# Attention scores from stacked float32r parts in place of zero-padded float32 operands

## What is computed

```
def _fox_attention(q, k, v, log_f):              # 8 heads of 64, causal, decay F
        s = jnp.einsum('bqhd,bkhd->bhqk', qi, k) * (HEAD_DIM ** -0.5)
        s = s + Fi[..., :, None] - F[:, :, None, :]
        s = jnp.where(kpos <= qpos, s, NEG)
        p = jax.nn.softmax(s, axis=-1)
        return jnp.einsum('bhqk,bkhd->bqhd', p, v)

def _swa_attention(q, k, v, sinks, rel_bias):    # 8 heads of 64, 2 groups of keys, window of 128
    logits = jnp.einsum('bnqhgd,bnkhd->bnhgqk', q, kb) * (HEAD_DIM ** -0.5) + bias
    p = softmax(concat([logits where valid, sink]))[..., :-1]
```

## Time and profile before

| | us |
|---|---|
| median of 3 runs | 3645.55 |
| lowest and highest | 3643.78, 3648.18 |
| the profiled execution's own time | 3645.56 |
| its span | 3643.8 |

### The profile page before, as it was taken

One profiled execution on the slowest core, in us unless ns is written; L12 is line 12 of the kernel. 1 busy time (PEld: TensorE's weight loads), 2 busy tenths in 40 slices (PEclk: granted clock), 3 DMA queues, 4 the chain that ended last, 5 costly groups with the idle time before them and its releaser, 6 DMA issues.

```text
span 3643.8 us, 49395 instructions
## 1 busy us (share of the span) xinstructions
PE 3344.9 (92%) x17315; PEld 2844.1 (78%) x17315; DVE 2569.9 (71%) x4990; ACT 1189.1 (33%) x2308; POOL 1856.8 (51%) x1095
## 2 busy tenths in 40 slices
PE   3999988888978778999999799999999999999997
PEld 3888766776857667888888688888888888888885
DVE  5111046652359998889889688888888887888888
ACT  3112135541122214666666322222222222222222
POOL 3991000004133433333333477777777777777776
PEclk8999989999989989999999899999999999999998
DMA  4443210013222113665666687888888888888885
GB/s 185 129 131 104 75 47 12 12 49 125 104 71 71 51 51 119 244 239 205 235 243 231 242 266 251 262 254 251 261 255 256 256 260 256 250 261 254 253 254 201
DMA packets 405835, 662.49 MB, mean 182 GB/s; under 512 B 219680, under 2 KB 270952, under 8 KB 402928
## 3 DMA queue, kind: packets, MB, share of 16 engines
q1 hardware_dynamic: 324656, 365.05, 31.4%
q0 software_dynamic: 78656, 286.30, 23.8%
q10 hardware_dynamic: 2304, 8.39, 0.6%
HBM read 564.21 MB, written 94.40 MB: 181 GB/s over the span
## 4 chain that ended last, share of the span: by engine, by line
PE 44%; DVE 10%; DMA 5%; POOL 1%; ACT 1%; issue 0%; SPq 0%; DVEq 0%; ACTq 0%; POOLq 0%
PE psum L2154 9%; PE psum L2155 9%; PE psum L2156 9%; PE psum L374 4%; PE psum L373 4%; PE psum L372 4%; DMA g_row<-in_expert_down,rows_of 4%; DVE g_hot L1850 4%; DVE g_hot L1829 2%; DVE g_row L1840 2%; DVE g_hot L1833 2%; POOL ga_downT_lo L1274 1%; PE psum L1282 1%; PE psum L1284 1%; PE psum L1283 1%
## 5 line engine op out<-in xcount | busy, mean ns | idle before, releaser
L2154 PE MATMUL psum<-e_u_hi,e_w_hi 128*128 128x512 f32 x1536 | 599.9, 391 | 16.7 <-POOL e_w_lo L2378 16.7
L2155 PE MATMUL psum<-e_u_lo,e_w_hi 128*128 128x512 f32 x1536 | 599.4, 390 | 0.0
L2156 PE MATMUL psum<-e_u_hi,e_w_lo 128*128 128x512 f32 x1536 | 598.6, 390 | 0.0
L2244 DVE TENSOR_TENSOR acc<-acc,psum 128x512 f32<-128x512 f32 x508 | 342.4, 682 | 248.0 <-PE psum L2156 232.9
L2260 DVE SCALAR_TENSOR_TENSOR acc<-e_row,e_row_weights,acc 128x1024 f32<-128x1024 f32 x256 | 468.7, 1831 | 10.2 <-DVE acc L2260 0.5
L2385 POOL TENSOR_TENSOR e_u_lo<-e_up,e_u_hi 128x1024 fp32r<-128x1024 f32 x128 | 388.8, 3038 | 16.3 <-ACT e_u_hi L2184 14.4
L2378 POOL TENSOR_TENSOR e_w_lo<-e_table,e_w_hi 128x768 fp32r<-128x768 f32 x128 | 247.4, 1933 | 249.9 <-ACT e_w_hi L2188 248.9
L2372 POOL DMA_INDIRECT e_row<-in_expert_up,rows_of x256 | 329.1, 1286 | 65.8 <-issue 53.3
L2154 PEld LDWEIGHTS psum<-e_u_hi,e_w_hi 128*128 128x128 f32 x1536 | 289.3, 188 | 75.7 <-POOL e_w_lo L2378 17.3
L2156 PEld LDWEIGHTS psum<-e_u_hi,e_w_lo 128*128 128x128 f32 x1536 | 289.1, 188 | 60.7
L2155 PEld LDWEIGHTS psum<-e_u_lo,e_w_hi 128*128 128x128 f32 x1536 | 289.4, 188 | 57.9
(11 more groups left out here) (277 smaller groups left out, 7919.5 us busy)
## 6 DMA issues: line engine op xcount, KB each, us to landing
e_up<-in_expert_up SPq DMA_DIRECT2D x128, 512.0 KB, 4.4
gate_table<-g_table SPq DMA_DIRECT2D x12, 4096.0 KB, 13.5
e_table<-gate_table SPq DMA_DIRECT2D x128, 384.0 KB
e_left<-in_expert_downT SPq DMA_DIRECT2D x59, 512.0 KB
e_left<-gelus_ahead SPq DMA_DIRECT2D x68, 384.0 KB
ga_downT<-in_expert_downT SPq DMA_DIRECT2D x49, 512.0 KB
gelus_ahead<-ga_gelu SPq DMA_DIRECT2D x48, 384.0 KB
pw_raw<-in_w_in SPq DMA_DIRECT2D x34, 512.0 KB
```

Of the source, the lines that this page charges most:

```text
L2154: nc.tensor.matmul(to, W_hi[:, q, rows], U_hi[:, q, cols], start=c == mine[0], stop=False)
L2155: nc.tensor.matmul(to, W_hi[:, q, rows], U_lo[:, q, cols], start=False, stop=False)
L2156: mm = nc.tensor.matmul(to, W_lo[:, q, rows], U_hi[:, q, cols], start=False, stop=c == mine[-1])
L2244: nc.vector.tensor_tensor(group(j), group(j), m.psum[:, 2 + J % BANKS], ALU.add).then_inc(acc_d, 1)
```

## The change

The scores are made of two float32r matmuls instead of one float32 matmul with zero padding. For a head, the keys' high part lies on its own half of the partitions and the low part on the other half (`kk`, `k_pair`). The queries' high part lies on both halves (`qh`), and so does their low part (`ql`). So the first matmul gives q_high times (k_high + k_low), the second q_low times the same. The mask is added by one float32r matmul, from copies `ident_r` and `mask_r`.

What makes these operands:
ScalarE scales the chunk of queries in place and waits for it, then rounds the high part of each head's queries and keys (`fox_high`, `stage_window`). GpSimd subtracts to get the low parts (`fox_low`); the window keys' low part is made by VectorE in the values stage. SP copies each of the three parts of a head to the other half of the partitions by DMA (`fox_pair`, `window`), 256 KB each. TensorE waits for these DMAs before a head's first job (`f_landed`, `w_landed`). `q_st`, `k_st`, `kdup` and their clearing are gone.

```diff
+def fox_high(nc, act, t, p, par):
+    c = p + 6
+    if par == 0:
+        nc.scalar.activation(t.qkvT[:, c], t.qkvT[:, c], ACT.Copy, scale=SCALE).then_inc(t.f_scaled, 1)
+        act.wait_ge(t.f_scaled, p + 1)
+    nc.scalar.activation(t.qh[0][par][half(par)], t.qkvT[half(par), c], ACT.Copy).then_inc(t.f_hi, 1)
+    nc.scalar.activation(t.kk[par][half(par)], t.qkvT[half(par), p + 10], ACT.Copy).then_inc(t.f_hi, 1)
+def fox_low(nc, pool, t, p, par):
+    pool.wait_ge(t.f_hi, p * 4 + (2 * par + 1))
+    nc.gpsimd.tensor_tensor(t.ql[0][par][half(par)], t.qkvT[half(par), p + 6],
+                            t.qh[0][par][half(par)].bitcast(F32), ALU.subtract).then_inc(t.f_lo, 1)
+    pool.wait_ge(t.f_hi, p * 4 + (2 * par + 2))
+    key = t.qkvT[half(par), p + 10]
+    nc.gpsimd.tensor_tensor(key.bitcast(F32R), key, t.kk[par][half(par)].bitcast(F32), ALU.subtract) \
+        .then_inc(t.f_lo, 1)
+def fox_pair(sp, t, p, par):
+    sp.wait_ge(t.f_hi, p * 4 + (2 * par + 1))
+    sp.dma_start(t.qh[0][par][half(1 - par)]..., t.qh[0][par][half(par)]...).then_inc(t.f_landed[par], 16)
+    sp.wait_ge(t.f_lo, p * 4 + (2 * par + 1))
+    sp.dma_start(t.ql[0][par][half(1 - par)]..., t.ql[0][par][half(par)]...).then_inc(t.f_landed[par], 16)
+    sp.wait_ge(t.f_lo, p * 4 + (2 * par + 2))
+    sp.dma_start(t.kk[par][half(1 - par)]..., t.qkvT[half(par), p + 10]).then_inc(t.f_landed[par], 16)
...
 values, SP
-            for g in range(2):
-                for half in range(2):
-                    sp.dma_start(t.kdup[...], t.qkvT[g * HD:(g + 1) * HD, 4])
+            fox_pair(sp, t, 0, 0)
...
+            fox_pair(sp, t, 0, 1)
+            for g in range(2):
+                sp.wait_ge(k_lo, g + 1)
+                sp.dma_start(t.k_pair[half(1 - g), g].bitcast(F32), t.qkvT[half(g), 4]).then_inc(k_landed, 16)
+            sp.wait_ge(k_landed, 32)
 values, ScalarE
+            fox_high(nc, act, t, 0, 0)
             act.wait_ge(fv, 1)
...
-            act.wait_ge(turned, 2 * len(vchunks))
-            for par in range(2):
-                nc.scalar.activation(first_q[par], t.qkvT[rows, 6], ACT.Copy, scale=SCALE)
+            act.wait_ge(turned, 4)
+            fox_high(nc, act, t, 0, 1)
+            for g in range(2):
+                nc.scalar.activation(t.k_pair[half(g), g], t.qkvT[half(g), 4], ACT.Copy).then_inc(k_hi, 1)
+            nc.scalar.activation(t.ident_r[:], t.ident[:], ACT.Copy).then_inc(consts, 1)
+            nc.scalar.activation(t.mask_r[:], t.mask[:], ACT.Copy).then_inc(consts, 1)
 values, GpSimd
-            for par in range(2):
-                nc.gpsimd.memset(t.q_st[(1 - par) * HD:(2 - par) * HD, :, par], 0.0)
-            nc.gpsimd.tensor_copy(t.k_st[:, 0], t.qkvT[:, 10])
+            for par in range(2):
+                fox_low(nc, pool, t, 0, par)
 values, VectorE, after the copies of v
+            for g in range(2):
+                dve.wait_ge(k_hi, g + 1)
+                nc.vector.tensor_tensor(key.bitcast(F32R), key, t.k_pair[half(g), g].bitcast(F32), ALU.subtract)
 attention, SP
             with sp.Fori(0, PAIRS - 1) as i:
+                window(i)
...
+                for par in range(2):
+                    fox_pair(sp, t, i + 1, par)
+            window(PAIRS - 1)
 attention, GpSimd
-                nc.gpsimd.tensor_copy(k_st[:, 1], t.kdup[:, i // 2]).then_inc(k_win, 1)
+                for par in range(2):
+                    pool.wait_ge(w_hi, i * 2 + (par + 1))
+                    nc.gpsimd.tensor_tensor(t.ql[1][par][half(par)], t.qkvT[half(par), i],
+                                            t.qh[1][par][half(par)].bitcast(F32), ALU.subtract).then_inc(w_lo, 1)
...
-                    nc.gpsimd.tensor_copy(k_st[:, 0], t.qkvT[:, i + 11]).then_inc(k_fox, 1)
+                    for par in range(2):
+                        fox_low(nc, pool, t, i + 1, par)
 attention, TensorE
-                    mm = nc.tensor.matmul(flat[:, o:o + x], q_st[:, br, par, n * P:(n + 1) * P],
-                                          k_st[:, br, k0 + h:k0 + h + x], start=True, stop=not diag)
+                    k = t.k_pair[:, i // 2, k0 + h:k0 + h + x] if br else t.kk[par][:, k0 + h:k0 + h + x]
+                    nc.tensor.matmul(flat[:, o:o + x], t.qh[br][par][:, n * P:(n + 1) * P], k, start=True, stop=False)
+                    mm = nc.tensor.matmul(flat[:, o:o + x], t.ql[br][par][:, n * P:(n + 1) * P], k,
+                                          start=False, stop=not diag)
-                        mm = nc.tensor.matmul(flat[:, o + x - P:o + x], t.ident[:], t.mask[:],
+                        mm = nc.tensor.matmul(flat[:, o + x - P:o + x], t.ident_r[:], t.mask_r[:],
 attention, ScalarE: stage(1, i, q_win) after job 0 becomes
+                nc.scalar.activation(t.qkvT[:, i], t.qkvT[:, i], ACT.Copy, scale=SCALE).then_inc(w_scaled, 1)
+                act.wait_ge(w_scaled, i + 1)
+                for par in range(2):
+                    nc.scalar.activation(t.qh[1][par][half(par)], t.qkvT[half(par), i], ACT.Copy).then_inc(w_hi, 1)
 and stage(0, i + 7, q_fox) after job FOX becomes
+                        for par in range(2):
+                            fox_high(nc, act, t, i + 1, par)
```

More of the change, by code:

```diff
@@ L571, in values @@
     negf_out = m.sem("v_negF_out")
-    first_q = [t.q_st[par * HD:(par + 1) * HD, 0, par] for par in range(2)]
+    k_hi = m.sem("v_window_key_high")
+    k_lo = m.sem("v_window_key_low")
+    k_landed = m.sem("v_window_key_landed")
+    consts = m.sem("v_consts")
     vchunks = [5, 14, 15, 16, 17]
@@ L648, in _ @@
                                           m.psum[:, 2 + u % 4].rearrange("p (i c) -> p i c", c=P)).then_inc(copied, 1)
+            for g in range(2):
+                dve.wait_ge(k_hi, g + 1)
+                key = t.qkvT[half(g), 4]
+                nc.vector.tensor_tensor(key.bitcast(F32R), key, t.k_pair[half(g), g].bitcast(F32), ALU.subtract) \
+                    .then_inc(k_lo, 1)
             dve.wait_ge(sinks, 16)
@@ L681, in attention @@
     flat = m.psum[:].rearrange("p b n -> p (b n)")
-    q_zero, q_fox, k_fox, negf_in = t.q_zero, t.q_fox, t.k_fox, t.negf_in
-    q_win = m.sem("at_staged_q_window")
-    k_win = m.sem("at_staged_k_window")
+    negf_in = t.negf_in
+    w_scaled = m.sem("at_window_scaled")
+    w_hi = m.sem("at_window_high")
+    w_lo = m.sem("at_window_low")
+    w_landed = [m.sem(f"at_window_pair_landed{i}") for i in range(2)]
     b_win = m.sem("at_staged_band")
@@ L750, in load, with window @@
                 sp.dma_start(nf[:, par], row.partition_broadcast(P)).then_inc(negf_in[par], 16)
+            def window(i):
+                for par in range(2):
+                    sp.wait_ge(w_hi, i * 2 + (par + 1))
+                    sp.dma_start(t.qh[1][par][half(1 - par)].bitcast(F32), t.qh[1][par][half(par)].bitcast(F32))                         .then_inc(w_landed[par], 16)
+                    sp.wait_ge(w_lo, i * 2 + (par + 1))
+                    sp.dma_start(t.ql[1][par][half(1 - par)].bitcast(F32), t.ql[1][par][half(par)].bitcast(F32))                         .then_inc(w_landed[par], 16)
             with sp.Fori(0, PAIRS - 1) as i:
+                window(i)
                 for par in range(2):
@@ L852, in copy, with stage_window @@
                 copies(act, lambda o, x: nc.scalar.activation(o, x, ACT.Copy), 0, copied_a, i, j)
-            def stage(br, c, sem):
+            def stage_window(i):
+                if not isinstance(i, int):
+                    hold(act, t)
+                nc.scalar.activation(t.qkvT[:, i], t.qkvT[:, i], ACT.Copy, scale=SCALE).then_inc(w_scaled, 1)
+                act.wait_ge(w_scaled, i + 1)
                 for par in range(2):
-                    rows = slice(par * HD, (par + 1) * HD)
-                    if not isinstance(c, int):
+                    if not isinstance(i, int):
                         hold(act, t)
-                    nc.scalar.activation(q_st[rows, br, par], t.qkvT[rows, c], ACT.Copy, scale=SCALE) \
-                        .then_inc(sem, 1)
+                    nc.scalar.activation(t.qh[1][par][half(par)], t.qkvT[half(par), i], ACT.Copy).then_inc(w_hi, 1)
             def pair(i, last):
@@ L2477, in build @@
         t.acc = m.at("acc", [P, TT, D], 84)
-        t.q_st = m.at("q_staged", [P, 2, 2, S], 140)
-        t.k_st = m.at("k_staged", [P, 2, S], 60)
         t.nf = m.at("negF_rows", [P, 2, S], 176)
-        t.q_zero = m.sem("q_staged_zeroed")
-        t.q_fox = m.sem("q_staged_fox")
-        t.k_fox = m.sem("k_staged_fox")
+        t.f_scaled = m.sem("fox_scaled")
+        t.f_hi = m.sem("fox_high")
+        t.f_lo = m.sem("fox_low")
+        t.f_landed = [m.sem(f"fox_pair_landed{i}") for i in range(2)]
         t.negf_in = [m.sem(f"negF_rows_landed{i}") for i in range(2)]
```

57 lines of the change are left out of this document (32 added, 25 removed).

## The result

The changed kernel takes 3666.28 us (median of 5 runs, 3664.74 to 3670.39) beside 3645.40 for the kernel before in the same comparison (5 runs, 3643.78 to 3648.18): ratio 1.0059, interval 1.0044 to 1.0074. It is 21 us slower; 7 us faster was forecast, and the time lies outside the predicted range. The profiled execution took 3667.33 us.

A forecast was written before the change was run, and what follows sets the result against it. TensorE's passes were taken to bound most fox jobs, a loop through several engines the window jobs. 3645.56 - 16.0 - 10.0 - 5.0 + 9.9 + 4.8 + 5.0 + 0.8 + 3.4 = 3638.5 us, range 3622 to 3655.

The forecast's parts named there:

- The pace of float32r: Score matmuls on TensorE: two float32r passes 512 wide cost 0.48 us against 0.86 for float32.
- the term of 16.0: Descending half of the fox jobs: TensorE never out of work, whole saving taken, 4 x 4.0 = 16.0 us.
- The ascending half: Ascending fox jobs: a loop through VectorE and ScalarE takes over, so 2.5 us a pair saved, 10.0 us in all.
- rival (c): Clock also falls at all four first jobs, into TensorE-bound work: 7 to 12 us more, 3646 to 3651; chance 0.12.
- the term of the clock: Falls of TensorE's clock behind the longer staging gaps, mainly the three window gaps: 5.0 us lost (0 to 12).
- rival (d): Clock stays at 1.2 GHz through window jobs, deciding once some 48 of 64 run so: 3654.5 us; chance 0.06.
- the 5.0 us of saving: Window jobs: shorter scores save 4 x 1.25 = 5.0 us (0 to 10.6), limited by VectorE's wait for the score.
- The staging: ScalarE's longer staging, all exposed: 3.3 us at three window places (9.9), 1.2 at four first jobs (4.8).
- the 0.8 us for contention: GpSimd's 52 us of subtractions disturbing VectorE: 0.8 us lost (0 to 4).
- The entry: Values stage up to the first score: that score comes at 498.8 us, 3.4 us later (2 to 6).
- the 5.8 set aside: The forecast's loss for TensorE's clock and GpSimd contention, +5.8 us, not assigned to any one part of the kernel.
- the three signs: Prediction wrong if window jobs fall under 1.35 us, TensorE waits for the doubled halves, or staging is hidden.

The follow-up runs named there:

- first experiment: Changed kernel with each window score as one float32 matmul, the q_low term left out, long staging kept: 3650.23 us, ratio 1.0023.
- rearranged kernel: Late-wait changed kernel, 1/8 scaling in projection copies, staging spread over four jobs, window scores one float32 matmul with unsplit queries: 3626.14 us, ratio 0.9955.
- rearranged kernel with the replaced denominator: That rearranged kernel with the window jobs' denominator as one tensor plus a per-partition scalar instead of a sum of two tensors: 3616.55 us, ratio 0.9932.
- third experiment: Kernel before with three more half-height ScalarE copies (3.15 us) behind its staging at the first window job, float32 passes kept: 3652.67 us, ratio 1.0031.

## Why the prediction was wrong

**The pace of float32r: right.** Score passes of 512 columns start 0.24 us apart (613.88 and 614.12). In the descending half TensorE's busy time went from 25.69 to 21.86 us, 3.8 of the 4.0 forecast, and the half itself got 3.15 us shorter:

```profile
602.72:625.26 22.54, 21.86 (x180) 20.82 (x180) 13.48 (x49) 11.56 (x24) 0.00 (x0) 1.00 0.08 24
```

The other 0.7 us became one wait for ScalarE's copy. At this pace four pairs give 12.6 us, so the term of 16.0 was 3 to 4 us too large.

**The ascending half: wrong, by the clock behind the change of pair.** The stretch from a pair's staging to its eighth maximum took 11.26 us in pair 2 of before and 13.74 and 13.19 in pairs 2 and 3 after, of which 1.2 was forecast for staging; the granted clock there is 0.63 and 0.61 for 1.00. With the window scores in float32 (first experiment) it takes 12.25 and 13.7 us, shorter in one pair and longer in the other, at 0.66 and 0.63. So this isn't, or not mainly, the low clock of the window jobs, which ahead of pair 2 of after has ended (1.00 at 585 to 588 us), but a fall of its own, rival (c)'s, which I had kept out of the sum: rows of after show 0.50 to 0.57 behind the staging of all four first jobs. The longer staging is not its only gap. At the turn of the loop TensorE is idle for 2.6 us without a wait that the profile shows (1.8 in before), and in the rearranged kernel, without staging in this place, the clock falls behind that gap as well. Where the clock holds, the saving is there. In the last pair of the rearranged kernel with the replaced denominator the first fox head takes 13.87 us at 1.00, from its first maximum to the end of its eighth, against 17.34 in before, also at 1.00. Up to 2.1 us of these 3.5 can come from the staging copies, which that kernel doesn't have there. So by my estimate the passes gave between 1.4 and 3.5 us, which doesn't contradict 2.5.

**The window jobs: wrong, in the term of the clock.** This is the step that failed first. I put 5.0 us (0 to 12) on the clock, from one fall that ended after 7 us, and took it that an end so soon belongs to the chip. It belonged to the float32 passes: with two float32r passes the three parts after have 27 to 34 us at half clock. The row could not show what shorter passes would do; but rival (d) had worked out the price, and its argument against ("after the fall in pair 0 the clock came back") was a row of the kernel with the longer passes. The point from which it decides, 48 of 64 jobs at half clock, was about met: 94 us of the three parts with staging (108 us) and 10 of the 25 us shown of the last pair. I also read the shallower gap too kindly. The clock stayed at 1.00 behind the one at 622 us, but before's third gap is as shallow (695 to 698 us, TensorE busy 1.64 of 3), and behind it stands:

```profile
698.00:701.00 3.00, 2.27 (x11) 1.99 (x12) 0.82 (x5) 1.36 (x7) 0.00 (x0) 0.73 0.00 0
```

And I searched for falls behind long gaps only; the last pair of after falls at its window jobs with no staging beside them. The price: window parts after are 2.6 to 3.7 us longer than with float32 passes, 9.5 us in three, and the 5.0 us of saving never came. The longer staging adds some 3.1 us in each part (5.2 for 2.1), 9.3 in three. The two together are 18.8 of the +21.6 us. By itself, in the kernel before, two float32r matmuls for each window score cost 0.35% against 0.04% with four, some 11 us.

**The staging: right.** 3.3 us a place was charged and all of it called exposed. The third experiment adds 3.15 us of copies and gets 3.2 to 5.0, a short fall of the clock included.

**GpSimd: right in its own times, wrong in what it does to others.** Its subtractions take 2.35 us (2.6 forecast) and no TensorE wait on the doubled halves appears in the attention stage. But the 0.8 us for contention spread it as a slowdown over all of VectorE's work. It is no slowdown spread over all instructions but a hold, seen here only on instructions with two tensor inputs in SBUF: some 3 us in the changed kernel, and some 8 us in the rearranged one, there with the clock's share. VectorE's maximum, with one operand in PSUM, isn't held (0.42 us at 560.13, beside a subtraction, as it takes elsewhere). The scan, also with two inputs in SBUF, takes 4.32 us beside the subtraction and 2.28 without it.

**The entry: right in kind, mis-sized.** Forecast 3.4 (2 to 6), measured 9.4. The shift by ScalarE is as worked out: the chain's sum starts at 483.22 for 481.32, 1.9 us (2.1 forecast). The scan adds 2.0. The rest, some 5.4 us, lies between the issue of the last copies and the first score (9.8 us for 4.4), and the stage waited for them: without SP's wait the first score comes 6.5 us sooner. I scaled 3.0 us down from a 512 KB copy of the attention stage and didn't look at what the queue holds in the values stage. That the large loads ahead are what delays these copies is not shown by a run.

Together: +21.6 for +6.2 in the window parts, -9.6 for -22.4 in the fox parts and the last pair, +9.4 for +3.4 at the entry, less the 5.8 set aside: 15.4 + 12.8 + 6.0 - 5.8 = 28.4 us between the two sums of the first table. None of the three signs by which the prediction would have called itself wrong came: TensorE didn't wait for the doubled halves in the attention stage, the staging wasn't hidden, and the window jobs grew instead of falling under 1.35 us. A sign for window jobs that get longer was missing.

## What to carry to other kernels

Before work of TensorE is shortened in a stretch that TensorE doesn't bound, ask whether that work is what holds its clock up; here two float32r matmuls more for each window score made a window part 2 to 4 us shorter. A row that shows the clock returning says so for the kernel with the old passes only. Beside GpSimd's subtractions look for VectorE instructions with two inputs in SBUF: they are held, not slowed. Where one input is a column, give it as a scalar. Price a DMA by the queue that it will stand in, not by its like in another stage.

## What the runs showed of the hardware

The granted clock stays at 0.50 through 10 us in which TensorE's records show 9.99 us busy (after, 570 to 580 us). In the kernel before with two float32r matmuls for each window score the window parts have 0.64, 0.64 and 0.61, with four 0.89, 0.94 and 1.00.

A VectorE sum of 128 x 1 with two inputs in SBUF took 154 ns alone and up to 2.2 us beside a GpSimd subtraction, ending within 0.02 us of it where the rows are shown; the same sum as tensor plus scalar took 0.21 us beside the same subtraction. Two long ones that overlap take turns: a scan 4.32 for 2.28 us, a subtraction 4.33 for 2.35. The Trainium skill's page "GPSIMD Engine Reference", in its table at the head, names two SBUF inputs as one condition for contention between the two engines. The trace agrees, and shows that the short instruction waits for the end of the long one.

A copy of 256 KB between partitions landed in 2.8 to 3.0 us (median) in the attention stage, and in 5.7 to 6.3 us in the values stage, where decay rows and biases are in the same queue.
